# Recurrent core of a hybrid decoder step: the head-masked spreads move from GpSimd to ScalarE

## The chip, the cores and the metric

The kernel runs on one core of a Trainium2 chip. The metric is device time in microseconds (us) of one execution. Three runs of the kernel before gave a median of 2888.62 us (2884.13 to 2890.76).

## The reference, cut to what matters

One inference step of a one-layer decoder for a prompt of 256 tokens and 8 samples of 8 tokens, all in fp32, with a width of 2048. The layer has a projection, an RWKV-7 recurrence of 16 heads of 64 beside a sparse attention, a cross attention and a mixture of 32 experts. The change touches the recurrence alone. Per head it is

```
def step(S, inp):
    r_t, k_t, v_t, kk_t, a_t, w_t = inp
    sa = einsum('bhij,bhj->bhi', S, -kk_t)
    S = S * w_t + sa[..., None] * (kk_t * a_t) + v_t[..., None] * k_t
    return S, einsum('bhij,bhj->bhi', S, r_t)
```

The kernel computes it in chunks: 16 tokens of the prompt, or the 8 tokens of a sample, make one chunk. For each chunk and head it needs a 64x64 map (what becomes of the state that enters) and a 64x64 term that is added. To get the maps of 8 chunks in one matrix multiply, an operand with the tokens on the partitions is repeated 8 times along the columns, and copy c is zero except in the rows of chunk c. These are the spreads.

## The kernel before, in words

The program is a row of stages, each a block that ends with a meeting of the engines: projection, selection and attention, `rwkv_prepare`, `rwkv_core`, `rwkv_finish`, output projection, cross attention, routing, experts, final norm. Stages do not overlap. The change is in `rwkv_core`.

`rwkv_core` goes through 12 quads (`quads()`): two halves of the heads, in each three token tiles in the order samples (64 tokens), prompt tokens 0 to 127, prompt tokens 128 to 255 (128 tokens each), and in each of these two quads of four heads. I number the quads 0 to 11: 0, 1, 6 and 7 have 64 tokens, the other eight 128. Into the steps of a quad are woven 8 places of the sequential state chain (`chain(gi, place)`) of the group before: a place holds a step of the state, and, where that group is the samples' (in quads 2, 3, 8, 9), also an export of a state and a load of the next one.

The order on each engine is the order of the program; engines meet by semaphores. In one quad:

- TensorE transposes four operands into two banks (L908); ScalarE takes them to `tm` (L749).
- TensorE makes the products within the chunks (L915, L923); VectorE masks them (L823, L828). TensorE and ScalarE begin `xx` (L931, L751, L754).
- Four rounds `it`: TensorE multiplies `xx` by the present power (L942) and squares the power (L946, L950); VectorE adds to `xx` (L834); ScalarE takes the squares to `pw` (L759): two takes in rounds 0 and 1, one in round 2.
- TensorE makes the maps (L958) from `xx` and the spread `bx`. It waits for the last add (L834) and for the four spreads (`bv_spread`). ScalarE takes the maps (L766).
- VectorE spreads `wx` (L839); TensorE makes the added terms (L965) from `tm` with `wx` and the spread `vx`; VectorE takes them (L843). TensorE makes the outputs (L974).

GpSimd makes `bx` and `vx`, four instructions a quad (L724), as soon as `tm` is taken and L965 of the quad before has ended (`add_made`). Behind them in its queue it issues the stores of exported states (L716, `send`), each after ScalarE's take of the export (L742, `so_read`). TensorE's load of the next state (L881) waits for that take too, as both use one bank:

```
if n["export"]:
    e.wait_ge(so_read, n["export"])
```

The rest of the code that the diff touches:

Of the kernel before, what the change touches and what calls it, by code (L numbers as in the profile page):

```python
# [9 lines left out]
ALU = mybir.AluOpType  # L10
ACT = mybir.ActivationFunctionType
# [3 lines left out]
P = 128  # L15
# [589 lines left out]
def rwkv_core(ph, I, O, R):  # L605
# [9 lines left out]
    nc, pool_dma_sem, sem, bank, cm, cw, pcol, prm, fr = ph  # L615
# [3 lines left out]
    with ExitStack() as tmp:  # L619
# [5 lines left out]
        tm = al("tm", [P, 2, 4, P])  # L625
# [5 lines left out]
        bx = al("bx", [P, 2, 8, P])  # L631
        vx = al("vx", [P, 2, 8, P])
# [10 lines left out]
    tm_made, tm_read, ab_made, ab_read = sem("tm_made"), sem("tm_read"), sem("ab_made"), sem("ab_read")  # L643
    akv_made, x_begun, xm_made, x_added = sem("akv_made"), sem("x_begun"), sem("xm_made"), sem("x_added")
    sq_made, sq_read, bv_spread, w_spread = sem("sq_made"), sem("sq_read"), sem("bv_spread"), sem("w_spread")
    map_made, map_read, add_read, qy_read = sem("map_made"), sem("map_read"), sem("add_read"), sem("qy_read")
    qy_made, add_made = sem("qy_made"), sem("add_made")
# [6 lines left out]
    E = 8  # L654
# [9 lines left out]
    def quads():  # L664
        for gi, (hg, ti) in enumerate(GROUPS):
            t0, m = TILES[ti]
            for q in range(2):
                yield 2 * gi + q, gi, hg, ti, t0, m, q, 4 * hg + 2 * q

    def parts(gi, place):  # L670

        if gi == 0:
            return
        hg, ti = GROUPS[gi - 1]
        c, odd = divmod(place, 2)
        if ti == 2:
            if odd:
                yield "step", gi - 1, c  # L680
            else:
                if c:
                    yield "export", gi - 1, c - 1
                yield "load", gi - 1, c
        elif odd:
            yield "step", gi - 1, c
        if place == 15 and ti:
            yield "export", gi - 1, c

    with nc.Block() as block:  # L690
        @block.sync
        def _(sp):
            n = 0
            sp.wait_ge(ends_ready, 2)
            for hg in range(2):
                for b in range(DB):
                    if n >= 2:
                        sp.wait_ge(si_turned, n - 1)
                    sp.dma_start(si[:, n % 2, :, :], I["state_wkv"][0, b, 8 * hg:8 * hg + 8].rearrange("h i j -> i h j")).then_inc(si_in[n % 2], 16)
                    n += 1  # L700

        @block.gpsimd
        def _(g):
            n = [0]

            def send(gi, places):

                for place in places:
                    for part, cg, c in parts(gi, place):
                        if part != "export":  # L710
                            continue
                        hg, b = EXPORTS[n[0]]
                        n[0] += 1
                        g.wait_ge(so_read, n[0])
                        dst = (O["wkv_p"][0, 0] if b is None else O["wkv_s"][0, b])[8 * hg:8 * hg + 8]
                        g.dma_start(dst.rearrange("h i j -> i h j"), so[:, (n[0] - 1) % 2, :, :].rearrange("i a (p j) -> i (a p) j", p=2)).then_inc(so_out[(n[0] - 1) % 2], 16)  # L716
            for k, gi, hg, ti, t0, m, q, hp in quads():
                em = cw("em16" if ti < 2 else "em8")[:m, 0:E].unsqueeze(2)
                g.wait_ge(tm_read, 2 * k + 2)
                if k:  # L720
                    g.wait_ge(add_made, k)
                for dst, col in ((bx, 1), (vx, 3)):
                    for p_ in range(2):
                        g.tensor_tensor(dst[:m, p_, 0:E, :], tm[:m, p_, col, :].unsqueeze(1).to_broadcast([m, E, P]),  # L724
                                        em.to_broadcast([m, E, P]), ALU.mult).then_inc(bv_spread, 1)
                send(gi, range(8 * q, 8 * q + 8))
            send(NGR, range(16))
            for i in range(2):
                g.wait_ge(so_out[i], 16 * (len(EXPORTS) // 2))

        @block.scalar
        def _(a):
            ns = 0
            n = [0]

            def chain(gi, place):
                for part, cg, c in parts(gi, place):
                    if part == "export":
                        a.wait_ge(so_turned, n[0] + 1)
                        if n[0] >= 2:  # L740
                            a.wait_ge(so_out[n[0] % 2], 16 * (n[0] // 2))
                        a.activation(so[:, n[0] % 2, :, :], bank[CHB][:HD, :].rearrange("i (a x) -> i a x", a=4), ACT.Copy).then_inc(so_read, 1)  # L742
                        n[0] += 1
            for k, gi, hg, ti, t0, m, q, hp in quads():
                for p_ in range(2):
                    a.wait_ge(tm_made, 2 * k + p_ + 1)
                    if k:
                        a.wait_ge(qy_made, k)
                    a.activation(tm[:m, p_, :, :], bank[p_][:m, :].rearrange("t (c x) -> t c x", c=4), ACT.Copy).then_inc(tm_read, 1)  # L749
                a.wait_ge(tm_read, 2 * k + 2)  # L750
                a.activation(xx[:m, :, 0:HD], tm[:m, :, 0, :].rearrange("t a (p j) -> t a p j", p=2), ACT.Copy).then_inc(x_begun, 1)  # L751
                chain(gi, 8 * q)
                a.wait_ge(akv_made, k + 1)
                a.activation(xx[:m, :, HD:P], bank[0][:m, 0:4 * HD].rearrange("t (h j) -> t h j", h=4), ACT.Copy).then_inc(x_begun, 1)  # L754
                for it in range(nit - 1):
                    chain(gi, 8 * q + it + 1)
                    for half in range(2 if it < nit - 2 else 1):
                        a.wait_ge(sq_made, ns + 1)
                        a.activation(pw[:m, it % 2, half, :, 0:m], bank[SQB[it][half]][:m, 0:4 * m].rearrange("t (h s) -> t h s", h=4),  # L759
                                     ACT.Copy).then_inc(sq_read, 1)  # L760
                        ns += 1
                for place in (4, 5):
                    chain(gi, 8 * q + place)
                a.wait_ge(map_made, k + 1)
                for p_ in range(2):
                    ins = a.activation(mts[:, gi % 2, 2 * q + p_, :, :], bank[MAPB[p_]][:, :].rearrange("p (c j) -> p c j", c=E), ACT.Copy)  # L766
                ins.then_inc(map_read, 1)
                for place in (6, 7):
                    chain(gi, 8 * q + place)
            for place in range(16):  # L770
                chain(NGR, place)
# [1744 lines left out]
```

## Time and profile before

| | |
|---|---|
| median of three runs | 2888.62 us |
| the profiled execution | 2886.18 us, its span 2884.4 us |
| mean granted clock of TensorE | 0.927 of full speed |
| TensorE matmul, busy share | 90% |
| VectorE, ScalarE, GpSimd, busy share | 26%, 16%, 6% |

The profile is of one execution. Busy shares of TensorE are of pipelined matmuls whose ends are modelled. A row of the timeline gives the start, the length, engine, line, operation, tiles and shapes, how many instructions it merges, and in brackets how long the engine sat idle before it and what released it. A row of the windows gives, for each engine, busy us and instructions in one stretch, then TensorE's granted clock (1.00 is 2.4 GHz, 0.50 is 1.2 GHz), the share of the DMA engines and GB/s.

### The profile page before, as it was taken

The page shows a single profiled execution, that of the slowest core. Times are in us where ns is not written, and L with a number is a line of the kernel's source. Part 1 is how long each engine was busy: PE and PEld are TensorE (multiplying, and loading weights), DVE is VectorE, ACT ScalarE, POOL GpSimd, SP SyncE. Part 2 cuts the span into 40 slices and gives each one's busy share as a digit, 9 for nine tenths or more (in the row PEclk, how much of TensorE's full clock was granted, in tenths as well). Part 3 has the DMA queues.
Part 4 walks back from the last instruction along what each step waited for, and adds up shares of the span by engine and source line. Part 5 has one row for each costly group of instructions (what it writes and reads, how often), then busy time and mean ns, then how long its engine had stood idle before and what let it go on. Part 6 is the DMA issues. An engine that isn't in the chain of part 4 may idle for free. (4 is left out here: it accounts for less than half of the span.)

```text
span 2884.4 us, 33985 instructions
## 1 busy us (share of the span) xinstructions
PE 2584.3 (90%) x13552; PEld 1417.0 (49%) x13552; DVE 755.6 (26%) x1378; ACT 450.1 (16%) x881; POOL 177.3 (6%) x180
## 2 busy tenths in 40 slices
PE   7999999999975788987599987799999999999996
PEld 4656765555543466665244554533443333344332
DVE  1046612122125355454310011311121112112113
ACT  2021022333323122121011021100000000000001
POOL 0000013001100223221000000000000000000000
PEclk9999999999986599697799997799999999999998
DMA  6513354777830010010433132399999999999996
GB/s 177 156 59 93 114 165 136 281 250 252 281 108 0 4 29 3 6 24 30 177 122 117 73 146 67 156 403 411 405 405 390 394 405 406 404 392 405 390 420 248
DMA packets 194083, 613.03 MB, mean 213 GB/s; under 512 B 37470, under 2 KB 104861, under 8 KB 142797
## 3 DMA queue, kind: packets, MB, share of 16 engines
q1 hardware_dynamic: 179581, 560.72, 50.6%
q0 software_dynamic: 10272, 35.96, 3.8%
q10 hardware_dynamic: 4080, 14.19, 1.3%
q8 instruction: 113, 1.85, 0.3%
q14 instruction: 37, 0.30, 0.0%
HBM read 599.61 MB, written 13.96 MB: 213 GB/s over the span
## 5 line engine op out<-in xcount | busy, mean ns | idle before, releaser
L346 PE MATMUL bank<-ht,w 128*128 128x320 f32 (+1 forms) x1888 | 566.8, 442 | 3.7 <-PEq L223 2.6
L2362 PE MATMUL bank<-wexp,fr 128*64 128x512 f32 x2048 | 445.5, 593 | 1.5 <-DVE fr L2273 1.5
L346 PEld LDWEIGHTS bank<-ht,w 128*128 128x128 f32 (+1 forms) x1888 | 341.9, 192 | 140.9 <-issue 30.5
L2362 PEld LDWEIGHTS bank<-wexp,fr 128*64 128x64 f32 x2048 | 146.0, 137 | 285.7 <-issue 284.7
L2415 PE MATMUL bank<-wexp,ut 128*64 128x512 f32 x1024 | 223.5, 594 | 11.3 <-ACT ut L2325 11.0
L2280 DVE TENSOR_TENSOR x<-x,bank 128x512 f32<-128x512 f32 x160 | 110.1, 688 | 376.1 <-PE bank L2374 368.0
L2415 PEld LDWEIGHTS bank<-wexp,ut 128*64 128x64 f32 x1024 | 72.1, 137 | 152.4 <-issue 136.4
L2342 PE MATMUL bank<-oh,hn 128*128 128x256 f32 x512 | 129.3, 396 | 8.2 <-DVE oh L2266 6.8
L1819 PE MATMUL bank<-wmix,fr 128*128 128x512 f32 x256 | 113.3, 604 | 18.8 <-DMA wmix<-in_w_out 18.8
L2374 PE MATMUL bank<-ys,sg 128*128 128x512 f32 x256 | 115.8, 606 | 2.0 <-ACT sg L2315 2.0
L2342 PEld LDWEIGHTS bank<-oh,hn 128*128 128x128 f32 x512 | 93.1, 192 | 46.3 <-issue 27.3
L1607 ACT ACTIVATE ktr<-bank 128x512 f32<-128x512 f32 x128 | 75.8, 597 | 104.5 <-PE bank L1548 104.0
L1819 PEld LDWEIGHTS bank<-wmix,fr 128*128 128x128 f32 x256 | 49.2, 194 | 81.3 <-issue 61.6
L2325 ACT ACTIVATE ut<-bank 128x512 f32<-128x512 f32 x16 | 9.6, 597 | 498.3 <-PE bank L2405 498.3
L1548 PEld LDWEIGHTS bank<-cm,kp 128*128 128x128 f32 x512 | 62.0, 143 | 42.6 <-issue 14.6
L2374 PEld LDWEIGHTS bank<-ys,sg 128*128 128x128 f32 x256 | 47.9, 192 | 69.0 <-issue 66.9
L1548 PE MATMUL bank<-cm,kp 128*128 128x128 f32 x512 | 80.0, 280 | 0.5 <-ACT ktr L1607 0.5
L2273 DVE TENSOR_TENSOR fr<-bank,gx 128x512 f32<-128x512 f32 x64 | 41.2, 686 | 135.2 <-PE bank L2345 135.2
L2302 DVE TENSOR_TENSOR u<-u,bank 128x512 f32<-128x512 f32 x16 | 11.0, 688 | 221.7 <-PE bank L2362 221.7
L2328 ACT ACTIVATE ys<-bank 128x512 f32<-128x512 f32 x64 | 33.0, 603 | 225.3 <-PE bank L2415 225.3
L724 POOL TENSOR_TENSOR bx<-tm,cm 128x1024 f32<-128x1024 f32 (+1 forms) x24 | 45.0, 1892 | 255.2 <-ACT tm L749 255.1
L942 PE MATMUL bank<-xx,pw 128*128 128x128 f32 (+1 forms) x288 | 50.0, 327 | 10.5 <-ACT pw L759 8.7
(412 smaller groups left out, 2741.1 us busy)
## 6 DMA issues: line engine op xcount, KB each, us to landing
wexp<-in_w_e SPq DMA_DIRECT2D x384, 1024.0 KB, 12.1
w<-in_w_in SPq DMA_DIRECT2D x29, 2048.0 KB, 8.9
kp<-in_cache_k SPq DMA_DIRECT2D x64, 512.0 KB, 5.4
vp<-in_cache_v POOLq DMA_DIRECT2D x64, 512.0 KB, 5.2
wmix<-in_w_out SPq DMA_DIRECT2D x3, 4096.0 KB, 13.2
wmix<-in_w_out SPq DMA_DIRECT2D x2, 2048.0 KB, 10.9
wmix<-in_w_ck SPq DMA_DIRECT2D x1, 4096.0 KB, 15.0
wmix<-in_w_cv SPq DMA_DIRECT2D x1, 4096.0 KB, 14.8
```

What stands on the lines that cost most here:

```text
L346: ins = e.matmul(self.bank[self.bank_no[n]][:width, 0:TOK], self.w[:, c % 2, k, j:j + width], self.ht[:, k, :], start=(k == 0), stop=(k == ...
L724: g.tensor_tensor(dst[:m, p_, 0:E, :], tm[:m, p_, col, :].unsqueeze(1).to_broadcast([m, E, P]), em.to_broadcast([m, E, P]), ALU.mult).then ...
L942: ins = e.matmul(bank[it % 2][:m, h * P:(h + 1) * P], up(h), xx[:m, h, :], start=True, stop=True)
L1548: ins = e.transpose(bank[g % 2][:, n * P:(n + 1) * P], kp[:, 4 * i + n, hp * P:(hp + 1) * P], cw("ident"))
L1607: a.activation(ktr[:, g % 8, :], bank[g % 2][:, :], ACT.Copy).then_inc(ktr_read, 1)
L1819: ins = e.matmul(bank[n % 4][:m, :], lhs(k), w[:, c % 2, k, :], start=(k == 0), stop=(k == KT - 1))
L2273: v.tensor_tensor(xg[buf][:, k:k + 3:2, :], bank[GB[i // 2][i % 2]][:, :].rearrange("p (k s) -> p k s", k=2), S["gx"][:, k:k + 3:2].unsque ...
L2280: v.tensor_tensor(xs, xs, bank[SB[i % 4]][:, :], ALU.add).then_inc(sc_read, 1)
L2342: e.matmul(bank[GB[j][i]][:, QS * y:QS * y + QS], hn[:, t, k * P:(k + 1) * P], oh[:, t, :], start=(t == 0), stop=False)
L2362: ins = e.matmul(half(bank[u // 4], a_), xg[buf][:, kk, P * h + SLOTS * a_:P * h + SLOTS * a_ + SLOTS], w[:, u % RING, a_, DE * k:DE * k + ...
L2374: ins = e.matmul(b[:, :], sg[:, t0:t0 + P], ys[:, CH * c:CH * c + CH], start=True, stop=True)
L2415: ins = e.matmul(half(bank[2 + c], a_), ut[:, f, SLOTS * a_:SLOTS * a_ + SLOTS], w[:, u % RING, a_, CH * c:CH * c + CH], start=(f == 0), s ...
```

## The change

GpSimd's four instructions a quad go, with their two waits; it keeps the stores of the exports. ScalarE makes each of the four spreads as 8 copies of 128 columns, each with a column of the mask `em` as scale for the partition: 32 copies a quad, 384 in all. Spread 0 follows the takes of the squares in round 0, spread 1 those of round 1, spreads 2 and 3 the one take of round 2. Only the last copy of a spread signals `bv_spread`, so TensorE's wait for 4 a quad stays as it is.

```diff
             for k, gi, hg, ti, t0, m, q, hp in quads():
-                em = cw("em16" if ti < 2 else "em8")[:m, 0:E].unsqueeze(2)
-                g.wait_ge(tm_read, 2 * k + 2)
-                if k:
-                    g.wait_ge(add_made, k)
-                for dst, col in ((bx, 1), (vx, 3)):
-                    for p_ in range(2):
-                        g.tensor_tensor(dst[:m, p_, 0:E, :], tm[:m, p_, col, :].unsqueeze(1).to_broadcast([m, E, P]),
-                                        em.to_broadcast([m, E, P]), ALU.mult).then_inc(bv_spread, 1)
                 send(gi, range(8 * q, 8 * q + 8))
...
+                em = cw("em16" if ti < 2 else "em8")
+
+                def spread(i):
+                    dst, col = ((bx, 1), (vx, 3))[i // 2]
+                    if i == 0 and k:
+                        a.wait_ge(add_made, k)
+                    for c in range(E):
+                        ins = a.activation(dst[:m, i % 2, c, :], tm[:m, i % 2, col, :], ACT.Copy, scale=em[:m, c:c + 1])
+                    ins.then_inc(bv_spread, 1)
                 for it in range(nit - 1):
                     chain(gi, 8 * q + it + 1)
                     for half in range(2 if it < nit - 2 else 1):
...
+                    spread(it)
+                spread(3)
                 for place in (4, 5):
                     chain(gi, 8 * q + place)
```

## Rows read from the trace of the kernel before

**Rows 1.** Windows, the recurrent core from its first to its last instruction.

```profile
949.00:1363.00 414.00, 349.18 (x3592) 268.46 (x3592) 196.32 (x428) 77.00 (x150) 102.55 (x66) 0.82 0.06 12
```

**Rows 2.** Line L724: durations min/median/max, and who waited for it (nobody is listed).

```profile
L724 POOL TENSOR_TENSOR bx<-tm,cm x24: 1884/1892/1897, 951.7 to 1310.1; 128x1024 f32<-128x1024 f32 x16, 64x1024 f32<-64x1024 f32 x8
...
who waited for it (us, times):
busy tenths in 40 slices 0000000000000223221000000000000000000000
```

**Rows 3.** Timeline of ScalarE: three scaled copies back to back; three plain copies.

```profile
1575.35 5.79 ACT L268 ACTIVATE xn<-x,stats 128x2048 f32<-128x2048 f32 x3
...
847.55 0.58 ACT L1637 ACTIVATE cd<-bank 26x128 f32<-26x128 f32 x3
```

**Rows 4.** Lines L268 and L1637: durations min/median/max in ns.

```profile
L268 ACT ACTIVATE xn<-x,stats x3: 1985/1986/2001, 1575.3 to 1579.1; 128x2048 f32<-128x2048 f32 x2, 64x2048 f32<-64x2048 f32 x1
...
L1637 ACT ACTIVATE cd<-bank x3: 252/255/266, 847.5 to 847.9; 104x128 f32<-104x128 f32 x2, 26x128 f32<-26x128 f32 x1
```

**Rows 5.** Groups of ScalarE by form: busy us, mean ns | idle before, releaser.

```profile
L1394 ACT ACTIVATE lg<-lg,sm 128x128 f32<-128x128 f32 x16 | 6.3, 394 | 17.8 <-DVE sm L1414 17.8
```

**Rows 6.** Timeline of ScalarE in quad 4: first take of round 1, take of round 2.

```profile
1093.69 0.60 ACT L759 ACTIVATE pw<-bank 128x512 f32<-128x512 f32 x1 [2.42 <-PE bank L946]
...
1097.39 0.60 ACT L759 ACTIVATE pw<-bank 128x512 f32<-128x512 f32 x1 [2.20 <-PE bank L946]
```

**Rows 7.** Timeline of TensorE in quad 4: maps, first added terms.

```profile
1100.36 1.94 PE L958 MATMUL bank<-bx,xx 128*64 128x512 f32 x8 [0.88 <-DVE xx L834]
...
1103.26 1.08 PE L965 MATMUL bank<-wx,tm 128*64 128x512 f32 x4
```

**Rows 8.** Timeline of ScalarE in quad 2: take of round 2, take of an export.

```profile
1030.06 0.60 ACT L759 ACTIVATE pw<-bank 128x512 f32<-128x512 f32 x1 [2.20 <-PE bank L946]
1032.61 0.59 ACT L742 ACTIVATE t<-bank 64x512 f32<-64x512 f32 x1 [1.96 <-PE bank L901]
```

**Rows 9.** Timeline of TensorE in quad 2: load of the next state, maps.

```profile
1033.46 0.43 PE L881 MATMUL bank<-cm,t 64*128 64x64 f32 x4 [0.88 <-ACT t L742]
1033.82 1.94 PE L958 MATMUL bank<-bx,xx 128*64 128x512 f32 x8
```

**Rows 10.** Timeline of ScalarE in quads 0 and 7: the take of round 2.

```profile
964.87 0.38 ACT L759 ACTIVATE pw<-bank 64x256 f32<-64x256 f32 x1 [2.97 <-PE bank L946]
...
1187.02 0.38 ACT L759 ACTIVATE pw<-bank 64x256 f32<-64x256 f32 x1 [2.97 <-PE bank L946]
```

**Rows 11.** Timeline of TensorE: maps of quad 0, round 2 of quad 6, maps of quad 7.

```profile
968.17 3.68 PE L958 MATMUL bank<-bx,xx 64*64 64x512 f32 x8 [0.84 <-DVE xx L834]
...
1148.48 1.97 PE L942 MATMUL bank<-xx,pw 64*64 64x128 f32 x8 [1.76 <-DVE xx L834]
...
1191.27 2.82 PE L958 MATMUL bank<-bx,xx 64*64 64x512 f32 x5 [0.87 <-DVE xx L834]
```

**Rows 12.** Groups of VectorE by form, 940 to 1345 us.

```profile
L804 DVE TENSOR_TENSOR t<-sta,ends 128x256 f32<-128x256 f32 x45 | 23.1, 514 | 0.1
L805 DVE TENSOR_TENSOR t<-t,nn 128x256 f32<-128x256 f32 x44 | 21.8, 496 | 1.5
...
L811 DVE TENSOR_TENSOR sta<-t,bank 128x256 f32<-128x256 f32 x28 | 11.8, 421 | 15.2 <-PE bank L893 14.9
```

**Rows 13.** Windows: two idle stretches of TensorE with what followed, and a slow stretch.

```profile
884.70:887.70 3.00, 0.01 (x1) 0.01 (x1) 2.46 (x2) 0.42 (x1) 0.00 (x0) 1.00 0.00 0
887.70:891.00 3.30, 3.30 (x7) 2.11 (x8) 1.17 (x3) 0.00 (x0) 0.00 (x0) 0.58 0.00 0
...
395.00:397.60 2.60, 0.02 (x2) 0.05 (x2) 0.00 (x0) 0.50 (x2) 0.00 (x0) 1.00 0.52 128
397.60:401.00 3.40, 3.40 (x15) 2.47 (x16) 0.00 (x0) 1.22 (x1) 0.00 (x0) 1.00 1.09 366
...
1052.00:1055.50 3.50, 3.50 (x18) 3.50 (x19) 1.45 (x3) 0.00 (x0) 2.95 (x3) 0.51 0.13 31
```

## The prediction

> **What bounds the kernel now.** I read the windows first, to find the stage: the recurrent core lasts 414 us, with TensorE busy for 349 of them at a mean clock of 0.82, and VectorE, ScalarE and GpSimd busy for 196, 77 and 103 [rows 1]. No stage runs beside it, so what it gains or loses goes into the time in full. Then line L724: its instruction takes 1.89 us, four a quad take 7.6, and nobody is listed as having waited for them [rows 2]. GpSimd's spreads are hidden whole. So the edit removes nothing that the end waits for, and the question is what 32 copies a quad cost ScalarE, and whether ScalarE has that room. The timelines of ScalarE and TensorE within a quad say so (their rows stand with the parts below). The reader is to see two things in them: up to L958 a quad is one chain (product, take, product, add, round after round) in which ScalarE waits for TensorE before each take; and after the take of round 2 only one product and one add are left before L958.
>
> **One copy.** Three scaled copies of 2048 columns take 5.79 us together and 1.99 each [rows 3, 4], so the second starts (5.79 - 1.99) / 2 = 1.90 after the first: neighbours overlap by 0.09. With a per-partition operand 128 columns take 0.394 [rows 5]. One copy therefore holds ScalarE for about 0.394 - 0.09 = 0.30 us. A spread of 8 holds it for 2.4, two in a row for 4.8, and two are finished 15 x 0.30 + 0.39 = 4.9 after they begin. Bounds: without that operand three copies of 128 columns take 0.58 together and 0.255 each, so 0.16 a copy [rows 3, 4]; without any overlap 0.39. I take 0.30, as L268 is the same operation with the same operands, back to back.
>
> **Spreads 0 and 1.** Each fits a wait that is there: 2.4 us against waits of 2.42 and 2.20 before the next take in a quad of 128 tokens [rows 6], which each begin when a take has just ended, and a copy can begin 0.09 before that. With exports between the takes, or with the 64 tokens of quads 0 and 1, the waits are longer. At most 0.1 is left over, on the take of round 2. Before it, spread 0 waits for L965 of the quad before, which is long done when the squares of round 0 are taken; nothing queues behind that wait.
>
> **Spreads 2 and 3.** They have no such wait to fill, and here the path pays.
> - Quads 4, 5, 10, 11. The take of round 2 ends at 1097.99 [rows 6]. Copies begin 0.09 earlier, plus the 0.1 left over, and end at 1098.0 + 4.9 = 1102.9; with the signal 0.05 later L958 can start. It started at 1100.36 [rows 7]: 2.6 late. L965 follows it after the maps and a step of the chain, on TensorE's own order, and is late by the same. 4 x 2.6 = 10.4.
> - Quads 2, 3, 8, 9. Behind the copies in ScalarE's queue stands the take of an export. The take of round 2 ends at 1030.66; ScalarE is free at 1030.66 - 0.09 + 0.1 + 4.8 = 1035.5, and the export's take began at 1032.61 [rows 8]: 2.9 late. TensorE's load L881 waits for that take, L958 stands behind L881 [rows 9], and VectorE's copy of the loaded state stands before its `wx`, so all move by 2.9. 4 x 2.9 = 11.6.
> - Quads 0 and 1. The take ends at 965.25 [rows 10], the copies at 965.25 - 0.09 + 4.9 = 970.06; L958 started at 968.17 [rows 11]: 1.9 late with the signal. 2 x 1.9 = 3.8.
> - Quads 6 and 7, where steps of the chain lengthen the rounds. Quad 7: 1187.40 - 0.09 + 4.95 = 1192.26 against 1191.27 [rows 10, 11], 1.0 late. In quad 6 a gain (next part) pays for its loss: 0.
>
> Sum on the path: 10.4 + 11.6 + 3.8 + 1.0 = 26.8 us.
>
> **What GpSimd gives back.** VectorE's L804 and L805 read two operands from SBUF. They take 0.42 us when GpSimd is idle, as L811 does, whose second operand is a bank; their sums are 23.1 and 21.8 where 45 and 44 of 0.42 make 18.9 and 18.5 [rows 12]. So 7.5 us of VectorE's time is stretched beside L724. Nearly all of it is off the path. In quad 6 it is not: TensorE sat idle for 1.76 us before L942 of round 2, released by VectorE [rows 11]. After the change that product still waits for the takes of round 1, which leaves about 1.0 of gain. The Trainium skill ("GPSIMD Engine Reference", Specifications) has the rule: GpSimd shares its SBUF interface with VectorE and gets in the way of VectorE's instructions that have two SBUF inputs. By it alone the change gains 7.5 us and not 1.0; this case's trace agrees on the stretch, and what it does to the end is a rival below. The stores of exports are no longer queued behind the spreads; ScalarE's takes of exports are released by TensorE and not by a store [rows 8], so that gives nothing.
>
> **The clock.** Before L958 TensorE sat idle for 0.88 us [rows 7, 9]. With the delay these stalls last some 3.5 us (0.88 + 2.6) and 3.8 (0.88 + 2.9) in the eight quads of 128 tokens, which run near full clock. The trace has longer idle stretches at full clock: after 3.0 us without a matmul the clock fell to 0.58 of full speed in the next stretch, after 2.6 us it stayed at 1.00 [rows 13]. The new stalls are on the side of the fall. A slow stretch in quad 3 lasted about 3.5 us at 0.51 [rows 13]; work bound by TensorE loses 3.5 x 0.49 = 1.7 us in it, and after L958 TensorE works without a break. Eight falls make 13.7. A part of a slow stretch can lie in the wait itself and costs nothing there, so I take 11; bounds are 0 (the clock holds) and 27 (two slow stretches each time). Quads 0, 1, 6, 7 mostly run at half clock already.
>
> **The sum.** 26.8 + 11 = 38 us on the profiled execution's 2886.2: 2924. The median of the runs shown is 2.4 us above that execution, so the forecast is 2926 us.
>
> **The rivals.**
> 1. The clock holds through the stalls: 27 us, 2915. For it: a stall of 2.6 left the clock alone; against it, the new ones are longer.
> 2. The falls last twice as long: 27 + 27 = 54, 2942. For it: the rows show one slow stretch of 3.5 us and do not say that a longer one is excluded; against it, the work after L958 is without a break.
> 3. Copies don't overlap, 0.39 each. Two spreads take 6.3 and spreads 0 and 1 overrun their waits by 0.7 and 0.9: about 5.3 late in each quad of 128, 3.3 in quads 0 and 1, 2 in 6 and 7, 53 with 14 for the clock: 2955. The overlap of L268 speaks against it.
> 4. Copies cost 0.16. Then L958 can start at 1100.8 (0.4 late, four times), the exports' takes are 0.6 late (four times), and quad 6 gains 1.0: 3 us, clock unmoved, 2891, within 0.2%. Against it: the operand's price in L1394.
> 5. Faster: the copies hide whole and the stretched VectorE instructions were on the path. The point is the exports' take: two spreads must pass in 1032.61 - 1030.57 = 2.0 us, so at 0.13 a copy or less. Then 7.5 us come back: 2881. Under the lower bound of a copy, and VectorE waits for TensorE behind most stretched instructions.
>
> **How the numbers follow.** Chances: the forecast 0.50, rival 1 0.17, rival 2 0.15, rival 3 0.08, rival 4 0.07, rival 5 0.03. I call a change of over 0.2% (5.8 us) what a measurement can tell from none. Faster: rival 5, 0.03. Same: rival 4, 0.07. Slower: the rest, 0.90. The range takes in rivals 1 and 2 with a few us on either side and leaves rivals 3 to 5 out, 0.18 in all: 2907 to 2947.
>
> **What would show it.** The new copies' row: 384 of about 0.39 us, starting 0.30 apart; twice 0.16 or 0.39 apart is rival 4 or 3. L958 in quad 4 about 4.9 us after the end of the round 2 take, released by ScalarE's copies; in quad 2 the export's take straight after the last copy, with L881 behind it. The windows of quads 2 to 5 and 8 to 11 with the clock lower by a tenth or more, and slow stretches of some 3.5 us behind the stalls; if it stays near full, rival 1. L804 and L805 at 0.42 throughout. The core at about 452 us in place of 414, and no other stage longer. The prediction is wrong if L958 is still released by VectorE's add, or if the time is under 2907.

## The result and the profile after

| | before | after |
|---|---|---|
| median of 4 runs each, us | 2886.38 (2883.51 to 2890.76) | 2928.87 (2920.36 to 2930.33) |
| ratio | | 1.0151, 95% interval 1.0126 to 1.0176 |
| profiled execution, its span, us | 2886.2, 2884.4 | 2929.95, 2928.1 |
| recurrent core in that span, us | 413.1 | 465.9 |
| everything else in that span, us | 2471.3 | 2462.2 |

The change is slower by 1.5% (36 to 51 us); forecast were 2926 us, 37 above the median shown before. The core grew by 52.9 us, the span by 43.7: the stages outside the core, whose code is the same, were 9 us shorter in this profile. In the eight experiments below they are the same code too, and lasted 2454.6 to 2472.6, so these 9 us are scatter between executions.

The core's window, as [rows 1] (PE, PEld, DVE, ACT and POOL busy, PEclk, DMA share, GB/s):

```profile
947.00:1414.00 467.00, 378.42 (x3592) 285.94 (x3592) 188.80 (x428) 187.50 (x534) 12.64 (x18) 0.76 0.06 11
```

TensorE has the same 3592 matmuls, but 378 us of them where there were 349, at a clock of 0.76 where it was 0.82. ScalarE went from 77 to 187 us with 384 more instructions; GpSimd lost 90. So there are two things to look for: where TensorE waits for ScalarE, and where its clock is lower.

The copies, grouped by form, against [rows 5] (busy us, mean ns, idle before):

```profile
L754 ACT ACTIVATE bx<-tm,cm 128x128 f32<-128x128 f32 x128 | 39.0, 392 | 0.0
L754 ACT ACTIVATE vx<-tm,cm 128x128 f32<-128x128 f32 x128 | 38.2, 396 | 0.0
```

ScalarE's timeline, the end of quad 2 and then quad 4, against [rows 8] and [rows 6] (start, length, then the instructions run together):

```profile
1033.83 0.59 ACT L760 ACTIVATE pw<-bank 128x512 f32<-128x512 f32 x1
1034.30 4.78 ACT L754 ACTIVATE vx<-tm,cm 128x128 f32<-128x128 f32 x16
1038.97 0.59 ACT L734 ACTIVATE t<-bank 64x512 f32<-64x512 f32 x1
...
1112.46 2.43 ACT L754 ACTIVATE bx<-tm,cm 128x128 f32<-128x128 f32 x8
1114.80 0.58 ACT L760 ACTIVATE pw<-bank 128x512 f32<-128x512 f32 x1
1115.27 4.77 ACT L754 ACTIVATE vx<-tm,cm 128x128 f32<-128x128 f32 x16
```

L760, L734 and L754 are the take of the squares, the take of the export and the copies. In each quad 16 copies run as one block of 4.78 us, so they start (4.78 - 0.395) / 15 = 0.292 apart. In quad 4 the take of round 2 ends at 1115.38 and the copies at 1120.04. In quad 2 the export's take starts 0.11 before the end of the block, 5.14 after the round 2 take started, where it had come after 2.55 [rows 8].

TensorE's timeline at the same places, quads 2 and 4, and quads 0 and 11 for the other two kinds, against [rows 7], [rows 9] and [rows 11] (in brackets its idle time and what ended it; L961 are the maps, L884 the load of the next state, L968 the added terms):

```profile
968.27 3.68 PE L961 MATMUL bank<-bx,xx 64*64 64x512 f32 x8 [2.73 <-ACT vx L754]
...
1039.82 0.66 PE L884 MATMUL bank<-cm,t 64*128 64x64 f32 x4 [3.50 <-ACT t L734]
1040.41 3.68 PE L961 MATMUL bank<-bx,xx 128*64 128x512 f32 x8
...
1115.70 1.16 PE L945 MATMUL bank<-xx,pw 128*128 128x128 f32 x8
1120.19 2.57 PE L961 MATMUL bank<-bx,xx 128*64 128x512 f32 x8 [3.33 <-ACT vx L754]
1124.51 1.97 PE L968 MATMUL bank<-wx,tm 128*64 128x512 f32 x4
1126.27 1.92 PE L968 MATMUL bank<-vx,tm 128*64 128x512 f32 x4
...
1374.11 3.53 PE L961 MATMUL bank<-bx,xx 128*64 128x512 f32 x8 [3.33 <-ACT vx L754]
```

Two things are to be seen. The releaser of the wait is no longer VectorE's add after 0.88 us [rows 7] but, ahead of the maps, the last copy after 3.33; with exports it is the export's take, ahead of L884, after 3.50 where it was 0.88 [rows 9]. And the eight maps that took 1.94 take 2.57 to 3.68, the added terms 1.97 instead of 1.08: behind the wait TensorE runs at half clock. Windows of the slow stretches behind the waits of quads 2, 4 and 5 say the same in numbers; the last row holds quads 2 to 4 with parts of their neighbours:

```profile
1039.40:1049.70 10.30, 9.88 (x54) 4.29 (x56) 4.20 (x9) 1.25 (x3) 0.72 (x1) 0.50 0.13 25
1121.40:1128.20 6.80, 6.80 (x46) 3.01 (x44) 0.56 (x2) 1.08 (x2) 0.00 (x0) 0.50 0.00 0
1155.50:1158.90 3.40, 3.40 (x10) 0.72 (x9) 0.94 (x3) 0.00 (x0) 0.00 (x0) 0.50 0.00 0
1011.00:1138.00 127.00, 104.16 (x998) 77.75 (x994) 55.34 (x121) 51.06 (x140) 5.65 (x8) 0.85 0.09 18
```

In the first three the clock is 0.50, the 1.2 GHz level, and TensorE is busy throughout but for 0.4 us in the first. The last has 998 matmuls at a mean clock of 0.85. The same window of the kernel before had 1221 at 0.97:

```profile
1011.00:1138.00 127.00, 108.47 (x1221) 85.29 (x1220) 67.03 (x145) 28.07 (x52) 35.48 (x24) 0.97 0.09 18
```

VectorE's L807 and L808, which stand against the groups of [rows 12], are at 0.42 throughout:

```profile
L808 DVE TENSOR_TENSOR t<-t,nn 128x256 f32<-128x256 f32 x48 | 20.4, 425 | 1.6
L807 DVE TENSOR_TENSOR t<-sta,ends 128x256 f32<-128x256 f32 x48 | 20.0, 416 | 0.1
```

Where the 52.9 us are, by the starting times in the two traces, from the start of a quad (its first take) to its maps, and from the maps to the next quad or, in quad 11, to the end of the core:

| quads | to the maps, growth (us) | forecast of the delay | behind the maps, growth |
|---|---|---|---|
| 4, 5, 10, 11 | 4.07, 3.58, 4.09, 2.45 | 2.6 each | 3.2, 1.65, 1.5, 2.3 |
| 2, 3, 8, 9 | 2.85, 2.84, 1.72, 2.84 | 2.9 each | 4.1, 2.2, 2.9, 2.15 |
| 0, 1 | 2.12, 3.64 | 1.9 each | 0, 0 |
| 6, 7 | -0.40, 3.02 | 0, 1.0 | 0, 0 |
| sum | 32.8 | 26.8 | 20.0 |

In quads 4, 5 and 10 a new slow stretch of 3.4 us lies early in the quad, long before the maps; in quad 8 one of before is mostly gone (3.4 us at half clock up to the maps, now 0.9); quads 1 and 7, which each held 3.4 us at full clock before, now run at half clock throughout. Without these, I estimate that about 26 of the 32.8 us are the delay and 7 the clock; with the 20 behind the maps, the clock's part is 27.

### The profile page after: what moved, and what is told of

Read it like the earlier page. It is cut to its first block and busy times, and to the rows that moved or that the text cites. A ratio compares the mean times of both kernels' runs of the same rounds, so it can differ in the third digit from the quotient of the medians.

```text
span 2928.1 us, 34310 instructions
## 1 busy us (share of the span) xinstructions
PE 2604.8 (89%) x13552; PEld 1429.0 (49%) x13552; DVE 747.9 (26%) x1378; ACT 560.7 (19%) x1265; POOL 87.0 (3%) x132
## 5 line engine op out<-in xcount | busy, mean ns | idle before, releaser
L1551 PEld LDWEIGHTS bank<-cm,kp 128*128 128x128 f32 x512 | 62.0, 143 | 42.5 <-issue 14.6
L961 PE MATMUL bank<-bx,xx 128*64 128x512 f32 (+1 forms) x96 | 40.7, 992 | 22.5 <-ACT vx L754 22.5
L754 ACT ACTIVATE bx<-tm,cm 128x128 f32<-128x128 f32 (+1 forms) x192 | 58.4, 391 | 0.0
```

The source lines that it names most:

```text
L754: ins = a.activation(dst[:m, i % 2, c, :], tm[:m, i % 2, col, :], ACT.Copy, scale=em[:m, c:c + 1])
L961: ins = e.matmul(half(bank[MAPB[h // 2]][:, :], h), xx[:m, h, 0:HD], bx[:m, h // 2, :, cols(h)], start=True, stop=True)
L1551: ins = e.transpose(bank[g % 2][:, n * P:(n + 1) * P], kp[:, 4 * i + n, hp * P:(hp + 1) * P], cw("ident"))
```

## The experiments

My theory: ScalarE's copies of spreads 2 and 3 keep the maps (and ahead of them the export's take) waiting, and the wait turns the clock down for the work behind it. Rivals: the amount of ScalarE's work, wherever it stands; spreads 0 and 1 as well; GpSimd or VectorE; slow stretches that have nothing to do with the wait. Medians, ratios to the kernel before on the same chip, and the core in the profile:

| kernel | median us | ratio, 95% interval | core us |
|---|---|---|---|
| after | 2928.87 | 1.0151 (1.0126 to 1.0176) | 465.9 |
| half_late | 2891.96 | 1.0028 (1.0011 to 1.0044) | 427.7 |
| half_early | 2917.96 | 1.0103 (1.0078 to 1.0128) | 456.9 |
| busy | 2917.05 | 1.0121 (1.0093 to 1.0150) | 453.1 |
| busy3 | 2914.56 | 1.0106 (1.0081 to 1.0132) | 443.7 |
| no_pool | 2884.52 | 0.9997 (0.9981 to 1.0013) | 418.6 |
| split | 2903.94 | 1.0070 (1.0050 to 1.0090) | 430.2 |
| split_late | 2882.86 | 0.9998 (0.9987 to 1.0009) | 410.9 |
| early | 2890.88 | 1.0023 (1.0007 to 1.0039) | 430.9 |

**half_late** makes every second copy in spreads 2 and 3 from quad 3 on (quads 0 to 2 whole), **half_early** the same in spreads 0 and 1. The pair takes away the same amount of ScalarE's work, 72 copies each, at two places.

```diff
-                    for c in range(E):
+                    for c in range(0, E, 2 if k > 2 and i >= 2 else 1):   # half_late
+                    for c in range(0, E, 2 if k > 2 and i < 2 else 1):    # half_early
```

> Left out: every second copy of spreads 2 and 3 from quad 3 on (8 of the 16 copies that follow the take of round 2), so the columns keep older values. Theory (the path pays for the copies behind the last take, and the stall they make lowers the clock): spreads 2 and 3 end 2.4 us earlier, L958 is at most 0.5 us late in quads 3 to 11, the stalls before it shrink to some 1.2 us and the clock holds there; quads 0 to 2 keep their loss of about 11. Core about 413 + 11 + 4 = 428 us, time about 2902. Rival (the whole load of copies on ScalarE costs, wherever it stands): a quarter of the copies is gone, so a quarter of the loss of 43 us: 2918.

> Left out: every second copy of spreads 0 and 1 from quad 3 on (8 of the 16 copies that lie between the rounds). Theory: these lie in waits that ScalarE has anyway, so nothing moves but the 0.1 to 0.5 us by which spread 1 overran: core 461 to 466 us as with the change, time 2922 to 2929. Rival (the whole load of copies costs): as much as with the late copies halved, 2918.

half_late, TensorE in quad 4, and the core's window:

```profile
1104.89 1.94 PE L961 MATMUL bank<-bx,xx 128*64 128x512 f32 x8 [1.00 <-ACT vx L754]
...
942.00:1370.00 428.00, 357.79 (x3592) 276.84 (x3592) 188.87 (x428) 166.41 (x462) 12.62 (x18) 0.80 0.06 12
```

half_early, TensorE ahead of and at the maps in quads 2 and 4, the window behind the stall of quad 2, and the core's window:

```profile
1038.41 0.43 PE L884 MATMUL bank<-cm,t 64*128 64x64 f32 x4 [3.50 <-ACT t L734]
1038.77 1.94 PE L961 MATMUL bank<-bx,xx 128*64 128x512 f32 x8
...
1114.29 2.68 PE L961 MATMUL bank<-bx,xx 128*64 128x512 f32 x8 [3.32 <-ACT vx L754]
...
1038.41:1050.60 12.19, 11.10 (x130) 6.53 (x131) 7.42 (x16) 1.68 (x4) 1.42 (x2) 1.00 0.23 44
...
946.70:1403.70 457.00, 369.10 (x3592) 282.96 (x3592) 188.82 (x428) 167.44 (x462) 12.67 (x18) 0.78 0.06 11
```

With half the copies the stall is 1.00 us, the maps behind it take 1.94 again, and the quads 3 to 11 grow by 0 to 0.3 us but for three (-1.4, 2.1, 1.7); 11 of the 14.6 us left are in quads 0 to 2, which still have all copies. The core came out at the 428 that I expected; the time, 2892, was 10 us under the 2902. With half of the early copies the delay is unchanged: 2.82 in quad 9, 2.43 in quad 11, 4.06 in quad 4, against 2.84, 2.45 and 4.07. The times alone would mislead here: half_early also came out 11 us below the change, under its forecast and at the time that I had given the rival. By quads that difference is clock: quad 2, whose copies were not touched, grew by 2.1 instead of 7.0, as no slow stretch fell behind its stall, which is 3.50 us as in the change. Quad 8 is the same. So it is the place of the copies, not their number; the slow stretches scatter by several us a profile, and a stall of this length is not followed by one every time.

**busy** and **busy3** leave all copies and give TensorE six, or three, matmuls more behind the product of round 3 (L942 of the kernel before), into a bank that nothing reads, so that it idles less in the wait.

```diff
+                    if it == nit - 1 and m == P:
+                        for _ in range(6):      # busy3: 3
+                            e.matmul(bank[0][:, :], ident, t1[:, 0:2, 0:P * 2], start=True, stop=True)
```

> Added to the changed kernel: six 512-column fp32 matmuls into a bank that nobody reads, behind L942 of round 3 in the eight quads of 128 tokens, 2.6 us of work for TensorE inside the stall. Theory: L958 starts as late as with the change (2.6 and 2.9 us), but the granted clock stays near full in quads 2 to 5 and 8 to 11, and the slow stretches of that part (about 20 us of the 53 by which the core grew) go: core about 443 us, time about 2906. Rival (the stalls do not bring the falls of the clock, or these cost nothing): no change or a loss by the added work, 2929 or more.

> The changed kernel with three (not six) 512-column fp32 matmuls into an unread bank behind L942 of round 3 in the quads of 128 tokens: by the run with six (5.32 us) they take 2.7 us, less than the stall, so that they don't lengthen it. Theory: L958 as late as in the change, no fall of the clock behind it, and only the lateness of the copies is left, 25 us, with some 6 for slow stretches early in a quad: core 438 to 446, ratio 1.010. Rival (the falls cost nothing): core 466, ratio 1.015.

busy, TensorE in quad 4 (L953 is the added work, L964 the maps), and the core's window:

```profile
1104.28 5.32 PE L953 MATMUL bank<-t,cm 128*128 128x512 f32 x12
1109.53 1.94 PE L964 MATMUL bank<-bx,xx 128*64 128x512 f32 x8
...
939.90:1393.00 453.10, 387.05 (x3688) 283.66 (x3688) 188.68 (x428) 187.53 (x534) 12.62 (x18) 0.84 0.06 11
```

busy3, the same, with the window from the maps of quad 4 to the next quad:

```profile
1110.00 2.74 PE L953 MATMUL bank<-t,cm 128*128 128x512 f32 x6
1113.50 1.94 PE L964 MATMUL bank<-bx,xx 128*64 128x512 f32 x8 [0.76 <-ACT vx L754]
...
1113.50:1123.00 9.50, 9.50 (x118) 5.67 (x119) 4.09 (x12) 1.08 (x2) 0.00 (x0) 1.00 0.01 2
948.80:1392.50 443.70, 374.99 (x3640) 283.67 (x3640) 188.70 (x428) 187.67 (x534) 12.63 (x18) 0.81 0.06 11
```

In busy I had mis-sized the added work: 5.32 us, not 2.6, so it ran past the end of the copies and became the delay itself (maps 3.5 to 5.8 late in the eight quads of 128 tokens); the core missed its forecast of 443 by 10 us and the time its 2906 by 11. In busy3 it fits, and the maps wait for the copies as in the change: 1.8 to 2.8 late in six of the eight quads of 128 tokens, about 3.9 in quads 4 and 11, which hold a new early slow stretch. In both kernels the time from the maps to the next quad is that of the kernel before in these quads (only in busy's quad 11 it is 0.8 us longer): no slow stretch follows the maps. So the fall of the clock behind the maps comes from the idle wait, not from the copies or from when they run. It is worth 465.9 - 443.7 = 22 us of the core between these two profiles, of which the 20 behind the maps are shown quad by quad. In time busy3 is at 1.0106, as expected, against 1.0151: the gap, some 13 us, has that sign, though the two intervals overlap a little.

**no_pool** is the kernel before with GpSimd's spreads made only in quads 0 and 2 (so that the buffers hold data of 64 and of 128 tokens), and TensorE waiting for those; no copies on ScalarE. It prices what GpSimd gives back.

```diff
-                g.wait_ge(tm_read, 2 * k + 2)
+                if k in (0, 2):
+                    g.wait_ge(tm_read, 2 * k + 2)
...
-                for dst, col in ((bx, 1), (vx, 3)):
+                for dst, col in ((bx, 1), (vx, 3)) if k in (0, 2) else ():
...
-                e.wait_ge(bv_spread, 4 * k + 4)
+                e.wait_ge(bv_spread, 4 if k < 2 else 8)
```

> The kernel before, in which GpSimd makes its spreads in quads 0 and 2 only and TensorE's waits count these; left out are the spreads of the other ten quads. It shows what GpSimd's absence gives by itself. Theory: L804 and L805 fall to 0.42 us, but only quad 6 had one of them on the path: 1 us, 2885 or so, not to be told from before. Rival (GpSimd was in the way of VectorE on the path): up to 7.5 us less, 2879.

no_pool, the two groups of VectorE of [rows 12], TensorE's product of round 2 in quad 6 (L942 in [rows 11]), and the core's window:

```profile
L806 DVE TENSOR_TENSOR t<-t,nn 128x256 f32<-128x256 f32 x48 | 20.4, 425 | 1.6
L805 DVE TENSOR_TENSOR t<-sta,ends 128x256 f32<-128x256 f32 x48 | 20.0, 416 | 0.1
...
1151.82 1.74 PE L943 MATMUL bank<-xx,pw 64*64 64x128 f32 x8 [0.56 <-ACT pw L760]
...
949.20:1367.90 418.70, 355.91 (x3592) 274.85 (x3592) 188.87 (x428) 76.99 (x150) 27.55 (x26) 0.80 0.06 12
```

The instructions are back at 0.42, and the time is level with before (0.9997). Quad 6 is 1.43 shorter, and of that 1.20 is the wait before L943, 0.56 instead of 1.76 us and now released by ScalarE; quads 3, 4, 5, 9 and 10 are the same within 0.04. The core as a whole is 5.5 longer, by other slow stretches in quads 0, 2 and 7 (1.8, 2.0, 2.1): that is how far this stage moved in one profile with nothing added to it.

**split** lets the maps wait for spreads 0 and 1 alone, which are all that they read, and puts the wait for spreads 2 and 3 ahead of the added terms. **split_late** also moves spread 3 behind ScalarE's steps 4 and 5 of the chain, and so behind the export's take.

```diff
-                e.wait_ge(bv_spread, 4 * k + 4)
+                e.wait_ge(bv_spread, 4 * k + 2)
...
+                e.wait_ge(bv_spread, 4 * k + 4)     # ahead of the added terms
...
-                spread(3)                           # split_late only
                 for place in (4, 5):
                     chain(gi, 8 * q + place)
+                spread(3)                           # split_late only
```

> The changed kernel, in which L958 waits for spreads 0 and 1 alone (it reads only these) and spreads 2 and 3 are waited for before L965. Theory (what costs is that L958 stands behind all 32 copies, and, with exports, that the take of the export does): quads 0, 1, 4 to 7, 10 and 11 are as long as before, as the copies end just before L965 would start (1102.9 against 1103.26 in quad 4); quads 2, 3, 8, 9 stay 2.9 us late with a fall of the clock behind three or four of the stalls. Core 413 + 11.5 + 5 to 10 = 430 to 435 us, ratio to before about 1.006. Rival (the load of the copies): as the change, 1.015.

> As the kernel with the divided wait, and the copies of spread 3 stand behind the takes of the exports of places 4 and 5. Theory: in quads 2, 3, 8, 9 the export's take is now 0.5 us late instead of 2.9, nothing else is late, quad 6 gains 1.4 us, no new falls of the clock: core 414 us, give or take 6 for the clock's slow stretches in the quads of 64 tokens; ratio to before 1.000, all 384 copies on ScalarE notwithstanding. Rival (load): 1.015.

split, ScalarE and TensorE in quad 2, the window behind its stall, and the core's window:

```profile
1030.68 4.81 ACT L754 ACTIVATE vx<-tm,cm 128x128 f32<-128x128 f32 x16
1035.38 0.59 ACT L734 ACTIVATE t<-bank 64x512 f32<-64x512 f32 x1
...
1036.22 0.43 PE L884 MATMUL bank<-cm,t 64*128 64x64 f32 x4 [3.53 <-ACT t L734]
...
1036.22:1048.41 12.19, 11.08 (x130) 6.52 (x131) 7.42 (x16) 1.68 (x3) 1.42 (x2) 1.00 0.23 44
949.10:1379.40 430.30, 356.11 (x3592) 273.01 (x3592) 188.65 (x428) 187.77 (x534) 12.67 (x18) 0.81 0.06 12
```

split_late, ScalarE in quad 2, TensorE in quad 4, and the core's window:

```profile
1030.76 2.46 ACT L754 ACTIVATE vx<-tm,cm 128x128 f32<-128x128 f32 x8
1033.10 0.59 ACT L734 ACTIVATE t<-bank 64x512 f32<-64x512 f32 x1
1033.58 2.46 ACT L754 ACTIVATE vx<-tm,cm 128x128 f32<-128x128 f32 x8
...
1099.52 1.94 PE L961 MATMUL bank<-bx,xx 128*64 128x512 f32 x8 [0.88 <-DVE xx L837]
...
948.20:1359.20 411.00, 346.70 (x3592) 266.24 (x3592) 188.85 (x428) 187.83 (x534) 12.66 (x18) 0.82 0.06 12
```

split takes the delay out of the quads without exports (0 in quad 5, 0.2 and 0.35 in quads 0 and 1; 1.6 in quads 4 and 10 by an early slow stretch) and leaves it in those with exports (2.2, 4.95, 2.1, 5.0), where L884 still waits 3.53 us for the export's take behind 16 copies. I had expected a fall of the clock behind three or four of these four stalls; there were two, in quads 3 and 9, which makes the difference between 2 and 5 us. split_late parts these copies, the take runs between them, and nothing of the loss is left: 0.9998, core 410.9, with all 384 copies on ScalarE and 187.8 us of its time. This settles that the loss came from the order, and from which spreads TensorE waits for ahead of the maps, and not from the work.

**early** moves each spread one place forward: spread 0 ahead of the quad's first step of the chain, spreads 1 to 3 behind the takes of rounds 0 to 2, so that one spread and not two stands behind the last take. TensorE's waits are those of the change.

```diff
+                spread(0)
                 chain(gi, 8 * q)
                 a.wait_ge(akv_made, k + 1)
...
-                    spread(it)
-                spread(3)
+                    spread(it + 1)
```

> The changed kernel with every spread one wait earlier: spread 0 in front of the take of the akv product (L754 before, L746 in the changed kernel), 1 and 2 behind the takes of rounds 0 and 1, 3 alone behind the take of round 2; the waits of TensorE as in the change. Theory: after the last take 2.4 us of copies remain, which is the time that L958 needs anyway: 0.2 us late in quads 4, 5, 10, 11, 0.5 in 2, 3, 8, 9 (export), 0.6 at the place 0 exports of quads 3 and 9, 0.7 in quad 6 for the akv take; together some 5 us, less 1.4 in quad 6. No falls behind L958. Core 417 us, ratio about 1.001. Rival (load): 1.015.

early, the core's window:

```profile
946.30:1377.30 431.00, 365.30 (x3592) 284.38 (x3592) 188.84 (x428) 188.02 (x534) 12.67 (x18) 0.78 0.06 12
```

No slow stretch follows the maps in any quad, and the time is 0.1 to 0.4% above before. The core missed its forecast (417): slow stretches early in quads 2, 3, 4, 5 and 11 cost 1.5 to 2.4 us each, and 3.3 in quad 6. Quads 0, 1 and 7 grew by 1.8, 0.6 and 2.1, as in no_pool, which has no copies. This profile was also the slow end of the kernel's runs (2884.84 to 2902.1). Whether those stretches come from the copies at a quad's beginning or from when the quad begins I can't say from it.

## Why the prediction was right, and where it was not

- **One copy: right.** 0.292 apart and 0.39 long, against 0.30 and 0.39. Rivals 3 and 4 fall on this row alone. L268, the same operation on 16 times as many columns, was the right row for the overlap. L1394, the row for the length, is an exponential with a bias for the partition and a sum, not a copy with a scale; its 0.394 fitted all the same.
- **Spreads 0 and 1 free: right.** Taking half of them away left the maps as late as in the change (half_early); in split the maps wait for nothing else, and quad 5 lost nothing.
- **Spreads 2 and 3: right, in both kinds.** Quads without exports 2.45 late for 2.6, by the last copy; quads with exports 2.84 for 2.9, by the export's take at the end of the block and L884 behind it; quad 0 2.1 for 1.9; quad 6 none. About 26 us for 26.8, and split and split_late take the two kinds away one after the other.
- **GpSimd's gift: right.** The stretch of VectorE is gone whole, and in no_pool 1.4 us of it reached the path, in quad 6, for 1.0. The 7.5 us that the Trainium skill's rule ("GPSIMD Engine Reference", Specifications) would give if every stretched instruction were on the path did not come; the rule itself agrees with the 0.42 that both instructions now take.
- **The clock: right in kind, wrong in size.** This is the term that was mis-sized. In the profile of the change the clock fell behind the stalls of 3.3 and 3.5 us in all eight quads, and busy3 shows that the stall is the cause. But I took 11 us and it was about 27, the end that I had called the bound. The price of one fall, 1.7 us, came from a single slow stretch of 3.5 us [rows 13]. Behind the new stalls four stretches lasted 6.8, one 10.2 and three 3.4, so the mean price was 20 / 8 = 2.5. The other 7 us are slow stretches before the maps, which I had not priced at all. For the core rival 2 was the better forecast: 413 + 54 = 467 against 465.9. And the step from [rows 13] to eight certain falls was luckier than it looks. The two waits shown there, 3.0 us with a fall and 2.6 without, do not part the cases: the same trace has another wait of 2.6 us with a fall behind it (the two rows under this list), and stalls of 3.5 us had none behind them in quads 2 and 8 of half_early and of split. So a stall of this length makes a fall likely here, and neither that it comes nor how long it lasts could be told from two rows.
- **The sum.** The core came out 14 us above my 452, and the total did not, since the rest of that execution was 9 us shorter than in the profile that I summed on. So the time of 2929 against 2926 is partly luck: the sum's larger term was right, its smaller one short by 16, and scatter between executions made up for most of that.
- **"No other stage longer": right**, none grew by more than 0.6 us.

The kernel before, a wait of 2.6 us of TensorE and the stretch behind it:

```profile
491.90:494.50 2.60, 0.03 (x2) 0.00 (x0) 0.00 (x0) 0.61 (x2) 0.00 (x0) 1.00 0.36 127
494.50:499.00 4.50, 4.45 (x11) 2.99 (x12) 1.40 (x3) 0.00 (x0) 0.23 (x1) 0.63 0.94 278
```

What stays open: why slow stretches begin some 5.5 to 7 us into a quad in some quads and not in others. Before the change they were in quads 3 and 9, after it in 3, 4, 5, 9 and 10, in split_late only in quad 2. A quad starts at another time in each run, with the same instructions on TensorE in it; whether that decides I can't say, as no run sets a quad's beginning alone. It is as open why the clock fell behind all eight stalls of the change, but not behind quads 2 and 8 of half_early and split.

## What to carry to other kernels

Room on an engine is not read from its busy share but from the wait in which the new work must fit: ScalarE had 80% of the stage free, two of four spreads fitted and two did not, and the same 384 copies cost 43 us or nothing by their order and by the place of TensorE's wait for them. Look at what stands behind added work in the engine's own queue (here the take of an export), and at which consumer really reads it (the maps needed two spreads of four). Where the delay becomes an idle wait of TensorE of some 3.5 us, price the clock behind it from several slow stretches, as one that may or may not come: in the profile of the change it cost as much as the delay, 27 us against 26.

## What the runs showed of the hardware

- A fall of the clock behind a stall of 3.3 to 3.5 us lasted 3.4, 6.8 or 10.2 us at 0.50, with TensorE busy in all of it or nearly so (9.88 of 10.30 us in quad 2); the length differed between quads with the same work. Behind stalls of 3.5 us in quads 2 and 8 of half_early and split there was none. After the shorter stall of half_late (1.00 us) there was none in quad 4.
- The core was 5.5 us longer with nothing added to it, through slow stretches at other places (no_pool). A per-quad comparison tells such a difference from an effect; one time does not.
- An added f32 matmul of 512 columns, with 128 columns of weights, stands twice in the trace: 5.32 / 12 = 0.44 us for each of the two (busy). The eight of the maps, with 64 columns of weights, took 1.94 together at the same full clock, but not because each is shorter: they start two at a time, as the first two in quad 4 of the change show (0.65 us for both, started 0.007 apart; in busy a pair follows the other after 0.43 us, as the added ones do). The two of a pair belong to different heads and write the two halves of a bank. I had sized busy's added work by the maps, and it came out twice as long.

```profile
1120.19 0.65 PE L961 MATMUL bank<-bx,xx 128*64 128x512 f32 x2 [3.33 <-ACT vx L754]
```
